# Second attention of a three-block kernel: the value products of a unit are issued ahead of the next unit's transposes

## What is computed

```python
# blocks of 128 queries; keys are the block before and the block itself (256)
scores = jnp.einsum("bnqkgd,bnskd->bnkgqs", qb, kb) * scale
scores = jnp.where(mask, scores, -jnp.inf)            # window of 128
sink = sinks.reshape(1, 1, N_KV_HEADS, GROUP, 1, 1)
m = jnp.maximum(jnp.max(scores, axis=-1, keepdims=True), sink)
p = jnp.exp(scores - m)
denom = jnp.sum(p, axis=-1, keepdims=True) + jnp.exp(sink - m)
p = p / denom
out = jnp.einsum("bnkgqs,bnskd->bnqkgd", p, vb)
# then: (out * silu(z)) @ w_out + b_out
```

## Time and profile before

| | us |
|---|---|
| median of 3 executions | 3140.32 |
| lowest, highest | 3138.95, 3142.75 |
| span of the profiled execution | 3139.1 |
| PE busy in it | 3048.2 (97%) |
| the second attention in it, first S to last V | 1795.84 to 1968.9 |

### The profile page before, as it was taken

How to read it: one execution, slowest core, us unless ns; L and a number is a source line. 1 busy time by engine, 2 the same in 40 slices (tenths; PEclk the granted TensorE clock), 3 DMA queues, 4 the chain that set the end, 5 groups by cost and what they waited for, 6 DMA issues and landing times.

```text
span 3139.1 us, 38243 instructions
## 1 busy us (share of the span) xinstructions
PE 3048.2 (97%) x15412; PEld 2443.9 (78%) x15412; DVE 1650.6 (53%) x2710; ACT 1155.6 (37%) x1971; POOL 964.1 (31%) x700
## 2 busy tenths in 40 slices
PE   8999989999999999999999999999999999999998
PEld 7876658887878888777888756778778878788877
DVE  6989661025546654233243587666655555533436
ACT  3125553222341121113332286445546323332334
POOL 2220002233417785124522122411111233342523
PEclk9999989999999999999999999999999999999999
DMA  4110001112422233113332210421011243443323
GB/s 137 47 36 19 14 14 47 48 54 108 135 62 86 86 105 95 44 47 134 108 116 61 56 55 28 161 76 34 22 47 48 92 110 94 141 139 109 108 74 108
DMA packets 252657, 243.75 MB, mean 78 GB/s; under 512 B 15776, under 2 KB 198048, under 8 KB 251456
## 3 DMA queue, kind: packets, MB, share of 16 engines
q1 hardware_dynamic: 231536, 197.10, 21.0%
q10 hardware_dynamic: 20944, 44.21, 4.3%
HBM read 200.83 MB, written 38.73 MB: 76 GB/s over the span
## 4 chain that ended last, share of the span: by engine, by line
PE 84%; DVE 6%; ACT 4%; DMA 3%; issue 1%; POOL 1%; SPq 1%; ACTq 0%; DVEq 0%
PE psum L561 23%; PE psum L563 23%; PE psum L562 23%; PE psum L567 3%; DMA arena<-in_w_in 2%; PE psum L744 1%; PE psum L770 1%; DVE arena L2915 1%; PE psum L1202 1%; PE psum L1153 1%; PE psum L1152 1%; PE psum L934 1%; ACT WS L1218 1%; PE psum L879 1%; PE psum L958 1%
## 5 line engine op out<-in xcount | busy, mean ns | idle before, releaser
L3214 POOL TENSOR_TENSOR WS<-arena,WS 128x1024 fp32r<-128x1024 f32 x279 | 692.7, 2488 | 1729.2 <-ACT WS L1218 1729.1
L561 PE MATMUL psum<-XH,WS 128*128 128x512 f32 x2600 | 1031.9, 397 | 16.2 <-ACT arena L2006 3.5
L563 PE MATMUL psum<-XH,WS 128*128 128x512 f32 x2600 | 1015.6, 391 | 0.0
L562 PE MATMUL psum<-XL,WS 128*128 128x512 f32 x2600 | 1014.9, 390 | 0.0
L561 PEld LDWEIGHTS psum<-XH,WS 128*128 128x128 f32 x2600 | 489.2, 188 | 134.3 <-issue 13.8
L563 PEld LDWEIGHTS psum<-XH,WS 128*128 128x128 f32 x2600 | 489.0, 188 | 103.5
L562 PEld LDWEIGHTS psum<-XL,WS 128*128 128x128 f32 x2600 | 489.5, 188 | 96.7 <-issue 0.7
L1218 ACT ACTIVATE WS<-arena 128x1024 fp32r<-128x1024 f32 x279 | 293.0, 1059 | 730.9 <-PE psum L563 255.3
L561 PE MATMUL psum<-WS,XH 128*128 128x512 f32 x960 | 378.1, 394 | 7.2 <-POOL WS L3214 5.1
L562 PE MATMUL psum<-WS,XH 128*128 128x512 f32 x960 | 374.9, 391 | 0.0
L563 PE MATMUL psum<-WS,XL 128*128 128x512 f32 x960 | 374.8, 390 | 0.0
(11 more groups left out here) (304 smaller groups left out, 3075.2 us busy)
## 6 DMA issues: line engine op xcount, KB each, us to landing
arena<-in_w_in SPq DMA_DIRECT2D x85, 512.0 KB, 3.8
arena<-in_w_out SPq DMA_DIRECT2D x48, 512.0 KB, 3.5
arena<-in_w_in_even SPq DMA_DIRECT2D x48, 512.0 KB, 4.3
arena<-in_w_out_even SPq DMA_DIRECT2D x32, 512.0 KB, 3.6
h_spill<-arena ACTq DMA_DIRECT2D x24, 512.0 KB, 3.1
arena<-s_table SPq DMA_DIRECT2D x8, 1536.0 KB, 6.8
arena<-in_w_in_odd SPq DMA_DIRECT2D x18, 512.0 KB, 3.9
s_table<-arena SPq DMA_DIRECT2D x32, 256.0 KB, 3.0
```

The source lines that it names most:

```text
L561: e.matmul(ps, wh, xh, start=start, stop=False)
L562: e.matmul(ps, wh, xl, start=False, stop=False)
L563: return e.matmul(ps, wl, xh, start=False, stop=stop)
L3214: e.tensor_tensor(lo, raw(book.raw_of.get(("w", u), 0), kbs, n), hi.bitcast(F32), SUB).then_inc(*w.up("w_lo", u))
```

## The change

Within a PE tick the two calls change places: V(u-3) is issued ahead of T(u-2). Nothing is added or removed, and no other engine's program changes.

```diff
             def tick(u):
                 if u < 32:
                     scores2(u)
+                if 3 <= u < 35:
+                    values2(u - 3)
                 if 2 <= u < 34:
                     turned2(u - 2)
-                if 3 <= u < 35:
-                    values2(u - 3)
```

## The result

The changed kernel takes 3146.01 us (median of 20 executions, 3141.69 to 3149.86) against 3140.61 for the kernel before on the same chip (20 executions, 3134.68 to 3147.63). The ratio is 1.0016, with a 95% interval of 1.0010 to 1.0023: 5.4 us slower, a loss that twenty executions just tell from nothing, and under the 0.2% that the prediction called a change. 3143 was predicted, with 3137.5 to 3148.5 as the range, so the loss is nearly twice the 2.9 us of the forecast.

A forecast was written before the change was run, and what follows sets the result against it. PE, busy 97% of the span, was taken as the bound in most ticks, DVE or ACT in a few. Terms -2.0 + 2.0 + 0.33 + 0.4 + 1.15 + 1.0 = +2.9 us on 3140.3 gave 3143 us, range 3137.5 to 3148.5.

The forecast's parts named there:

- V does not fill the wait: PE's waits for divide: V needs a bank freed by the gate queued behind divide; first product comes 0.24 us later.
- (a): PE's changes of array tile: S to V takes 1.06 us; each tick bound by PE gets 0.17 us shorter.
- (b): Ticks 9, 13, 17: later T delays copies and powers, so PE's filler starts 0.67 us later each; +2.0 us.
- (c): Ticks 10, 14, 18, where PE waits for DVE: gate's start to F's start grows 0.11 us each; +0.33 us.
- (e): Tick 28: later T delays powers(28), then POOL and DVE, which has no slack; +1.15 us.
- (f): The end, ticks 32 and 33: V(30) waits first and T(31) comes behind it; +1.0 us.
- (g): Twelve ticks free of chains (3, 6, 7, 11, 15, 19 to 24, 31): 0.17 us less each; -2.0 us.
- (d): Ticks 19, 21, 23: V waits some 0.14 us each behind the emptying of bank 7; +0.4 us.
- The clock: Rival: longer PE waits lower TensorE's clock, 1.4 to 2 us per fall; chance 0.12 for three or more, 0.15 for fewer.
- main forecast: Whole kernel: the summed terms, without clock falls, give +2.9 us, 3143 us; chance 0.40.
- one or two falls: Case of TensorE's clock falling behind one or two PE waits; two falls give 3146.5 us; chance 0.15.
- The sign: Whole kernel: "same", within about 0.2% (6.3 us), chance 0.83; slower 0.13, faster 0.04.

The follow-up runs named there:

- e1: Changed kernel with DVE's gate moved earlier, between weigh(u) and divide(u-1), as gate(u-3); 3137.98 us.
- e5: Changed kernel with T back ahead of V in ticks 8, 12 and 16; 3142.19 us.
- e6: Changed kernel with T back ahead of V in tick 28 and from tick 32 on; 3142.37 us.
- e3: Changed kernel with the score products of units 10 and 14 issued twice, same result; 3143.70 us.
- e4: Kernel before, with V ahead of T only in ticks 3, 6, 7, 11, 15, 19 to 24 and 31; 3139.39 us.
- e8: Changed kernel with T back ahead of V in ticks 10 and 14; 3143.12 us.
- e11: Changed kernel with DVE's gate between weigh and divide, and T ahead of V in ticks 8, 12, 16 and 23; 3133.54 us.
- e2: Kernel before (T ahead of V) with only DVE's gate moved earlier, between weigh and divide; 3147.81 us.

## Why the prediction was right

**V does not fill the wait.** Right, and the heart of it: the resource that V lacks is freed behind the divide in DVE's own order. V started 0.46 us after the gate's start (0.47 was taken), and e1, which differs from the changed kernel in the gate's place alone, takes 3138.0 against 3146.0.

**(a)** Right. S to V is 1.06 us, which no row of before had shown; the lower bound of 0.86 is out, and a tick in which V waits for nothing is some 0.17 shorter (4.51 us for tick 11; 4.52 was forecast). The rule of the Trainium skill, page "TensorEngine Tiling (Array Packing)", Key Properties, says that a change of mode drains TensorE. The trace agrees as far as that a gap stands at this change too, from 64x128 to 128x64, some 1.06 - 0.86 = 0.20 us by the pace of the other products; that it is a drain no run here shows.

**(b)** Right in the mechanism (e5: the waits go back from 1.23 to 0.52). Its size was taken as 0.67; ticks 8 and 9 together are 0.52 us longer than before. The copies came 1.0 us later after S, but the first exponential started 0.97 us after the start of the two copies, and not the 1.09 that they are listed with.

**(c), (e), (f)** Right in the mechanism. In e5, where the clock stays up in tick 14, it is 2.33 us from the start of the gate (1861.54) to that of F, against 2.23 before: 0.10 for (c), where 0.11 stood. e6 gives 0.85 for the order of tick 28, where 1.04 stood, and 0.86 for the end, where 1.0 stood: both some 0.15 to 0.2 us too large.

**(g) with (d)** This is the term of the sum that was mis-sized: forecast for S(19) to S(29) was -0.6, measured 0.0. Ticks 19 to 24 do what they were to do: the even ones gain 0.17 each, the odd ones 0.08, since V waits for the bank there (d), which costs 0.1 and not 0.14; together -0.77. But they were called free of chains, and tick 23 is not: powers(23), the two weight blocks behind it and POOL's 4.73 us hang on it, and DVE is the bound from there to tick 28. Ticks 25 to 28 gave 0.78 back. I had looked for the chain only where PE's filler waits for L1716, and missed the one where DVE waits for POOL. Errors in (b) and (e) go the other way, and that is luck: without it the sum without the clock, 5.98 - 3.2 = 2.8 us, would not agree with +2.9 so well.

**The clock.** The main forecast had none of its falls; what happened is the case of "one or two falls", which had a chance of 0.15 and 3146.5 us. The wait of tick 14 was worked out as 2.04 us and came as 1.93; the fall cost 1.6 us each, within the 1.4 to 2 of the prediction. The step that failed is the weight given to it: a wait longer than the 1.71 us that had left the clock alone, and about as long as the 2.04 us behind which it had fallen, was given about one chance in four (0.15 and 0.12), where the runs (below) show seven falls in ten such waits. So the measured 3146.0 lies in the range because the range took that case in, and not because the main sum holds it.

**The sign.** "Same" was the most likely class, and the time moved within it, and toward the side to which the sum leaned; by nearly twice as much.

## What to carry to other kernels

Before a product is moved into a wait, read what its own operands and its PSUM bank wait for, in the *order of the engine that frees them*: here the bank was freed by an instruction queued directly behind the one that was being waited for. Two orders that must meet (PE's and DVE's) are changed together or not at all. And a wait on TensorE has a second price besides its length: here, when one grew from 1.7 to 1.9 us, the products behind it ran at the lower clock in most cases, which cost another 1.6 us.

## What the hardware showed beyond that

- **Waits and the clock.** Waits of PE in ticks 10 and 14, over the kernels above: up to 1.71 us the clock never fell (before, e1, e3, e4, e8 to e11). Of ten from 1.92 us up (changed 1.94, 1.93; e6 1.95, 1.94; e5 1.92, 1.94; e2 2.16, 2.17 and, in tick 33, 2.55; and tick 2 with its 2.04, counted once, though all twelve kernels have that wait and the clock fell behind it in each) it fell behind seven. It did not behind e5's 1.94 in tick 14, e2's 2.16 in tick 10 and its 2.55 in tick 33. In the first two the filler's wait just ahead was 0.52 us, in the changed kernel and in e6 1.23 or 1.24; but with 0.52 ahead it fell as well, behind e5's 1.92 and e2's 2.17. So the length of the wait alone does not decide at about 2 us. What else does is open.
- **The scatter of the times goes with the clock.** Over the 86 executions of the kernel before that were timed beside the experiments, those with a mean granted clock of 0.992 have a median of 3138.4 us, with 0.991 3139.7, with 0.990 3142.1 and with 0.989 3145.2. That is a correlation and was not tested.
- **DVE stands still beside POOL.** In rows 7 the operation L2802 on 128x4 values takes 1.19 us and ends with POOL's, where it takes 0.16 with POOL idle; L2804 took 2.32 us in the changed kernel and L2812 2.30 in e2. The Trainium skill, page "GPSIMD Engine Reference", Specifications, says that the two engines share their interfaces to SBUF and contend for them when DVE has two SBUF inputs or runs in a two-port mode. The trace agrees: of the first kind are L2802 and L2812 with two inputs. L2804 and L2817 have one and were held as well (four L2817: 3.15 us against 1.14); whether they run in a two-port mode no run here shows.
